# A routed expert layer: two gathers and two stores under way, a new order of issue on GpSimd, the router by token tiles, and the first expert loads in the norm before it

## The reference, cut to what matters

```python
p_group = softmax(h @ w_rg + b_rg)              # 4 groups, the best one is taken
p_top, g_idx = top_k(p_group, 1)
e_top, e_local = top_k(expert logits of that group, 2)   # 8 experts in a group
weights = p_top * softmax(e_top)
# each token's row goes to its two experts, in padded blocks of one expert
def expert_block(args):
    xb, e = args
    return (silu(xb @ w_gate[e]) * (xb @ w_up[e])) @ w_down[e]
out = sum over the two experts of weights * y
```

## Time and profile before

| what | us |
|---|---|
| median of 3 runs | 3223.88 (3222.1 to 3224.71) |
| the profiled execution, its time | 3233.42 |
| its span in the trace | 3231.7 |
| PE busy | 2530.7 (78%) |
| DVE, ACT, POOL busy | 1255.3, 944.7, 364.4 |
| mean granted PE clock | 0.879 of full |

### The profile page before, as it was taken

The page is one execution under the profiler, slowest core; times in us unless marked ns, Lnnn a source line. Parts: engine busy times, 40 slices in busy tenths (PEclk is TensorE's granted clock), DMA queues, the critical chain, the costliest instruction groups (busy, mean ns, idle before and its releaser), DMA issues. The chain is left out here.

```text
span 3231.7 us, 51558 instructions
## 1 busy us (share of the span) xinstructions
PE 2530.7 (78%) x17988; PEld 1959.7 (61%) x17989; DVE 1255.3 (39%) x2672; ACT 944.7 (29%) x1720; POOL 364.4 (11%) x706
## 2 busy tenths in 40 slices
PE   4974698589889859699898388894969998658883
PEld 4963688445445438476677266663847677636662
DVE  3447334311111145447443432235734753432224
ACT  2233323112112122236322133332234532213232
POOL 0000000012111110000000233231000000113233
PEclk9987899789999979799999598896979999768887
DMA  3201231489999942122121669944122121289972
GB/s 119 80 1 39 66 117 53 181 354 407 414 409 412 404 153 75 33 66 66 50 57 56 276 234 348 349 182 139 53 57 58 49 63 44 65 347 363 362 298 100
DMA packets 208903, 565.75 MB, mean 175 GB/s; under 512 B 26198, under 2 KB 170198, under 8 KB 184192
## 3 DMA queue, kind: packets, MB, share of 16 engines
q1 hardware_dynamic: 191056, 538.71, 45.1%
q0 software_dynamic: 17712, 25.23, 2.4%
HBM read 560.18 MB, written 35.92 MB: 184 GB/s over the span
## 5 line engine op out<-in xcount | busy, mean ns | idle before, releaser
L997 PE MATMUL ps<-e_wgu,e_xT 128*64 128x128 f32 (+1 forms) x2688 | 426.4, 321 | 41.2 <-issue 22.5
L997 PEld LDWEIGHTS ps<-e_wgu,e_xT 128*64 128x64 f32 x2688 | 344.4, 147 | 165.2 <-issue 116.7
L999 PE MATMUL ps<-e_wgu,e_xT 128*64 128x128 f32 (+1 forms) x2688 | 426.1, 321 | 0.0
L999 PEld LDWEIGHTS ps<-e_wgu,e_xT 128*64 128x64 f32 x2688 | 344.0, 147 | 0.0
L1020 PE MATMUL ps<-e_wd,e_hidT 128*64 128x512 f32 x1112 | 303.8, 682 | 5.4 <-ACT e_hidT L1051 4.0
L1903 PE MATMUL ps<-t_hT,t0a_t0g_w 128*128 128x512 f32 x768 | 199.2, 411 | 4.6 <-DVE t0a_t0g_w L1925 2.4
L1903 PE MATMUL ps<-t_hT,t1a_t1g_w 128*128 128x512 f32 x768 | 198.0, 409 | 4.6 <-DVE t1a_t1g_w L1925 2.4
L1162 DVE COPY e_y_out<-e_y 128x512 f32<-128x512 f32 x108 | 46.3, 429 | 372.9 <-DMA e_dram_y<-e_y_out,e_choicecur 267.4
L447 POOL TENSOR_TENSOR all_x<-all_x,ln_rows 128x1024 f32<-128x1024 f32 x16 | 48.2, 3040 | 1262.5 <-DVE all_x L440 1262.5
L1170 DVE TENSOR_TENSOR e_hid<-e_silu,ps 64x128 f32<-64x128 f32 (+1 forms) x210 | 67.1, 334 | 299.5 <-ACT e_silu L1048 293.0
L1048 ACT ACTIVATE e_silu<-ps 64x128 f32<-64x128 f32 (+1 forms) x210 | 63.9, 304 | 378.5 <-PE ps L999 377.5
(11 more groups left out here) (604 smaller groups left out, 4738.6 us busy)
## 6 DMA issues: line engine op xcount, KB each, us to landing
e_wgu<-in_w_exp_gate_up SPq DMA_DIRECT2D x54, 2048.0 KB, 9.2
e_wgu<-in_w_gate_up SPq DMA_DIRECT2D x22, 4096.0 KB
e_wd<-in_w_down SPq DMA_DIRECT2D x32, 2048.0 KB
e_wd<-in_w_exp_down SPq DMA_DIRECT2D x64, 1024.0 KB
m_both<-in_w_gate_up SPq DMA_DIRECT2D x10, 4096.0 KB, 37.8
r_hT<-in_w_exp_gate_up SPq DMA_DIRECT2D x10, 2048.0 KB
t0a_t0g_raw<-in_w_in SPq DMA_DIRECT2D x32, 512.0 KB
t1a_t1g_raw<-in_w_in SPq DMA_DIRECT2D x32, 512.0 KB
```

The source lines that it names most:

```text
L997: nc.tensor.matmul(ps_gu[q][0:SLOTS], xT[:, c, :], wgu[s][:, 0, c, span], start=c == 0, stop=c == DC - 1)
L999: last = nc.tensor.matmul(ps_gu[q][SLOTS:P], xT[:, c, :], wgu[s][:, 1, c, span], start=c == 0, stop=c == DC - 1)
```

## The change

- `ExpertRing` and `Router` are new: the ring of weights and the router's tiles belong to the stage around the norm and the expert layer. The norm's SP program loads the router and the first 2 (e0) or 5 (e1, e2) experts. In `moe` SP first stores the rows, and then, after the logits and the store, loads the last slot.
- The logits: 32 matmuls with a 128x128 tile of `hT` stationary and the router's 36 columns moving, no copy on ACT and no turning back.
- The counts have a semaphore of their own and are multiplied ahead of the ranks; the numbers of blocks come by rounding (3 instructions for 7). The tables that the loops read, the softmax weights and the scaling of x come later on DVE. `tokcol` comes ahead of `choicecol`, and POOL gathers as soon as `tokcol` is there; the small stores come behind two gathers, and are four.
- `landing` and `y` have two buffers each, `y_out` is gone; DVE copies the result from PSUM straight to `y`, ACT doesn't.
- DVE's order in block g: both `hid`, `xT`, the result's copy, `stage_rows`. PE turns the first half of the hidden rows ahead of the next block's rows.
- POOL goes by pairs of blocks, rounded up: store of block n, then gather of block n+3 into the buffer of block n+1. With an odd number of blocks one empty store and gather are added.
- The results come back tile by tile, both halves of a tile in turn.

```diff
@@ rms_rows / post_norm, SP @@
+                if ring is not None:
+                    ring.load_first(sp)
...
+                if router is not None:
+                    for dst, src in router.loads:
+                        sp.dma_start(dst, src).then_inc(router_landed, 16)
+                    ring.load_first(sp)
+                    sp.wait_ge(router_landed, 16 * len(router.loads))
@@ ExpertRing @@
+    def load_first(self, sp):
+        for s in range(self.n - 1):
+            for m in range(2):
+                self.load(sp, s, s, m)
@@ moe, SP @@
-                first = [(s, m) for s in range(RING) for m in range(2)]
-                for s, m in first[:EARLY]:
-                    load(s, s, m)
-
-                for n in range(EARLY, len(first)):
-                    if n == 2 * OWN:
-
-                        sp.wait_ge(logitsT_ready, 1)
-                        sp.wait_ge(rows_stored, 16)
-                    load(first[n][0], *first[n])
+                sp.wait_ge(logits_ready, 1)
+                sp.wait_ge(rows_stored, 16)
+                for m in range(2):
+                    ring.load(sp, RING - 1, RING - 1, m)
@@ moe, PE @@
-                pe.wait_ge(router_landed, 64)
-
-                for c in range(DC):
-                    last = nc.tensor.matmul(ps[0:NG + NE, 6, :], router[:, c, :], hT[:, c, :], start=c == 0, stop=c == DC - 1)
-                last.then_inc(logitsT_ready, 1)
-                pe.wait_ge(logitsT_copied, 1)
                 for t in range(TT):
-                    last = nc.tensor.transpose(ps[:, t, 0:NG + NE], logitsT[:, t * P:(t + 1) * P], ident[0:NG + NE, 0:NG + NE])
+                    for c in range(DC):
+                        last = nc.tensor.matmul(ps[:, t, 0:NG + NE], hT[:, c, t * P:(t + 1) * P], router.w[:, c, :],
+                                                start=c == 0, stop=c == DC - 1)
                 last.then_inc(logits_ready, 1)
...
+                        turn_hid(g, 0)
                         pe.wait_ge(rows_staged, g + 2)
                         turn()
...
+                        turn_hid(g, 1)
@@ moe, ACT @@
-                        act.wait_ge(y_ready, g + 1)
-                        act.wait_ge(y_moved, g + 1)
-                        nc.scalar.copy(y[:], ps_y).then_inc(y_copied, 1)
@@ moe, DVE @@
                         g = dve.snap(done)
-                        move_y(g)
                         for q in range(2):
                             dve.wait_ge(silu_ready, g * 2 + (q + 1))
                             vec.tensor_tensor(hid[SLOTS:P, q], silu[SLOTS:P, q], ps_gu[q][SLOTS:P], ALU.mult).then_inc(hid_ready, 1)
                         turn_copy(g + 2)
-                        stage_rows(g + 2)
+
+                        dve.wait_ge(y_stored[0], (g + 4) // 2 * 16)
+                        dve.wait_ge(y_stored[1], (g + 3) // 2 * 16)
+                        dve.wait_ge(y_ready, g + 1)
+                        vec.tensor_scalar(y[:, bass.ds(g % 2, 1)].rearrange("p one d -> p (one d)"), ps_y,
+                                          1.0, None, ALU.mult).then_inc(y_copied, 1)
+
+                        dve.wait_ge(rows_gathered[0], (g + 4) // 2 * 16)
+                        dve.wait_ge(rows_gathered[1], (g + 3) // 2 * 16)
+                        vec.tensor_scalar(gathered[:], landing[:, bass.ds(g % 2, 1)].rearrange("p one d -> p (one d)"),
+                                          1.0, None, ALU.mult).then_inc(rows_staged, 1)
@@ moe, POOL @@
-                        pool.wait_ge(rows_staged, g + 3)
-                        gather(g + 3)
-
-
-                        pool.wait_ge(y_moved, g + 2)
-                        nc.gpsimd.tensor_copy(choicecur[:], choicecol[:, bass.ds(g, 1)]).then_inc(choicecur_ready, 1)
+                with pool.Fori(0, n_pairs) as pair:
+                    for p in range(2):
+                        n = pair * 2 + p
+                        pool.wait_ge(y_copied, n + 2)
+                        store(n, p)
+                        pool.wait_ge(rows_staged, n + 2)
+                        gather(n + 3, 1 - p)
```

More of the change, by code:

```diff
@@ L318, in plain, with rms_rows @@
     return f
-def rms_rows(nc, name, parts, eps, loads=()):
+def rms_rows(nc, name, parts, eps, loads=(), ring=None):
     with Stage(nc, name) as st:
@@ L872, in moe @@
         y_copied = st.sem("y_copied")
-        y_moved = st.sem("y_moved")
-        y_stored = st.sem("y_stored")
+        y_stored = [st.sem(f"y_stored{n}") for n in range(2)]
         back_landed = [st.sem(f"back_landed{n}") for n in range(2 * TT)]
@@ L980, in turn, with turn_hid @@
                     last.then_inc(turned, 1)
+                def turn_hid(g, q):
+                    pe.wait_ge(hid_ready, g * 2 + (q + 1))
+                    for f in range(HF):
+                        last = nc.tensor.matmul(ps_hid[q][:, f * SLOTS:(f + 1) * SLOTS],
+                                                hid[SLOTS:P, q, f * P:(f + 1) * P], ident[SLOTS:P, SLOTS:P],
+                                                start=True, stop=True)
+                    last.then_inc(hid_turned, 1)
                 pe.wait_ge(rows_staged, 1)
@@ L1090, in _ @@
                 vec.tensor_copy(gpad[:, 0, 0:1], diff[:, 0:1]).then_inc(diff_ready, 1)
+                dve.wait_ge(counts_ready, 1)
+                blocks = rounded([nblk[:, n] for n in range(3)], ps[:, 5, 0:NE], 1.0 / SLOTS, 0.5 - 0.5 / SLOTS, 1.0)
+                link(vec.tensor_tensor_scan(ends[:, 0], blocks, blocks, 0.0, ALU.add, ALU.bypass))
+                link(vec.tensor_tensor(ends[:, 1], ends[:, 0], blocks, ALU.subtract))
+                link(vec.tensor_scalar(ends[:, 2], ends[:, 1], float(SLOTS), None, ALU.mult))
@@ new lines, in _ @@
+                dve.wait_ge(rank_ready, 1)
+                link(vec.tensor_tensor(slot[:], ps[:, 4, 0:TT * NE].rearrange("p (t e) -> p t e", e=NE),
+                                       ends[:, 2:3].to_broadcast([P, TT, NE]), ALU.add))
+                for j in range(2):
+                    link(vec.tensor_tensor(picked[:, j], slot[:], hot[:, j], ALU.mult))
+                link(vec.tensor_reduce(slotf[:], picked[:].rearrange("p j t e -> p (j t) e"), AX_X, ALU.add))
+                in_block = rounded([blk[:, n] for n in range(3)], slotf[:], 1.0 / SLOTS, 0.5 / SLOTS - 0.5)
@@ new lines, in _ @@
+                vec.tensor_tensor(flat, flat, k["choice"][:].rearrange("p j t -> p (j t)").unsqueeze(2).to_broadcast(
+                    [P, 2 * TT, TABLE]), ALU.mult).then_inc(hot_slots_ready, 1)
+                vec.tensor_copy(table[0:1, 0], blocks[0:1]).then_inc(table_ready, 1)
+                vec.tensor_copy(table[0:1, 1], ends[0:1, 0])
+                n_pairs = rounded([pairs[:, n] for n in range(3)], ends[0:1, 0, NE - 1:NE], 0.5, 0.25)
+                vec.tensor_copy(pair_table[:], n_pairs).then_inc(table_ready, 1)
@@ new lines, in _ @@
+                dve.wait_ge(tokT_ready, 1)
+                vec.tensor_scalar(part[:, 0], ps_tok, 1.0, float(4 * S + 2), ALU.is_lt, ALU.mult)
+                link(vec.tensor_scalar(part[:, 1], ps_tok, float(S), float(-S), ALU.is_gt, ALU.mult))
+                link(vec.scalar_tensor_tensor(part[:, 3], ps_tok, -1.0, part[:, 1], ALU.add, ALU.add))
+                vec.tensor_tensor(tokcol[:], part[0:SLOTS, 3], part[0:SLOTS, 0], ALU.add).then_inc(tokcol_ready, 1)
+                link(vec.tensor_scalar(part[:, 2], ps_tok, 2.0, k["second"][:], ALU.mult, ALU.add))
@@ L1134, in _ @@
-                vec.tensor_tensor(tokcol[:], part[0:SLOTS, 3], part[0:SLOTS, 0], ALU.add).then_inc(tokcol_ready, 1)
+                if alpha != 1.0:
+                    dve.wait_ge(rows_stored, 16)
+                    link(vec.tensor_scalar(x[:], x[:], alpha, None, ALU.mult))
                 def turn_copy(n):
@@ new lines, in _ @@
+                pool.wait_ge(rows_stored, 16)
+                pool.wait_ge(landing_cleared, 1)
+                pool.wait_ge(tokcol_ready, 1)
+                for n in range(2):
+                    gather(n, n)
+                for n in range(4):
+                    nc.gpsimd.dma_start(spare_dram[n:n + 1], ident[0:1, 0:SLOTS]).then_inc(y_stored[n % 2], 16)
+                pool.wait_ge(choicecol_ready, 1)
+                pool.wait_ge(rows_staged, 1)
+                gather(2, 0)
+                pool.wait_ge(table_ready, 2)
@@ L1229 @@
+                n_pairs = pairs_of_blocks(pool)
+                with pool.Fori(0, n_pairs) as pair:
[5 more added lines that the diff above has]
+                        gather(n + 3, 1 - p)
+                for n in range(2):
+                    pool.wait_ge(rows_gathered[n], n_pairs * 16 + 32 - 16 * n)
 class Columns:
```

317 lines of the change are left out of this document (136 added, 181 removed).

## The result

The changed kernel takes **3254.0 us** (median of 4 runs, 3248.5 to 3260.6) against 3223.0 before: ratio **1.0102**, interval 1.0075 to 1.0129. It is 31 us slower. The forecast was 3166, and the range ended at 3215. The profiled execution took 3260.6 us, span 3258.8, which is 27.1 us more span than before.

What follows compares the result with a forecast made beforehand. Weights bound e0's loop; in e1 and e2 PE waits for `hid`, with DVE late at a store. Prologues -43.5, loops -13 and -3, ends +1.7 sum to -58: median 3166 us, range 3105 to 3215.

Steps and rivals of the forecast that it cites:

- the term L: Expert loops: a gather's landing time behind a store, taken as 7.2 us, the mean of 6.2, 8.0 and 7.5.
- The sum for a pair: Loops of e1 and e2: two blocks take L + 8.5 us plus 2 x 1.33 for the clock, 18.4 in all.
- a gain of 13 us: Loops of e1 and e2: 9.2 us a block against 9.47, over some 48 blocks, -13 us.
- Rival B: Loops: the gather lands late behind its store, beside loads that never pause; L = 11, 3256 us; chance 0.09.
- the prologues at -43.5: Serial part ahead of each expert loop: e0 -14.4, e1 -14.8, e2 -14.3 us, sum -43.5.
- Rival C: Prologues: router matmuls stay at the lower clock, first gather still meets loads; -16 instead of -43.5, 3193 us; chance 0.17.
- Rival A: Loops: shorter stalls leave the clock up, loads then bound a block at 8.3 us; 56 us gained, 3123; chance 0.27.
- The logits: Router in the prologue: 22 records at the lower clock, 42 at the higher, 10.3 us; change 0, bounds -3.6 and +3.9 a layer.
- The early loads: Prologue: weights loaded from the norm on shorten the first gather's landing by 5.0, 4.5, 4.0 us; rows stored behind them cost nothing.
- e0's counts in full: e0's prologue gain of 14.4 us counts whole, since 430 us of saturated loading follow.
- The end: End of each layer: -0.7 us each without ACT, up to +3.8 for e2's empty store and gather; sum +1.7.

Runs made afterwards that it cites:

- Experiment 10: Changed kernel, but in e1 and e2 the next expert's gate-and-up load is issued at an expert's last block's end, with the down load: 3221.5 us, ratio 0.9976.
- experiment 3: Light loads: ring refills bring only 1/16 of gate and up and 1/16 of down (1/32 in e0), store still ahead of gather: 2953.3 us, one run.
- experiment 2: Changed kernel with the gather issued ahead of the store, but both waits kept ahead of both issues: 3154.0 us, ratio 0.9791.
- experiment 9: Changed kernel with e2's stores issued but all half rows except one out of bounds, results read back from the stored rows: 3257.0 us, one run.
- experiment 8: On top of experiment 1, the first experts' loads moved back into the expert layer, behind the rows' store: 3127.5 us, ratio 0.9702.
- Experiment 4: The changed kernel's new prologue with the loop of before (one landing buffer, result copied by ScalarE, gather ahead of store): 3187.6 us, ratio 0.9903.
- experiment 1: Changed kernel with gather n+3 issued ahead of the store of block n, without waiting for that block's end: 3110.8 us, ratio 0.9656.

## Why the prediction was wrong

**The loop's structure was right, the term L was mis-sized.** The sum for a pair was L + 8.5 + 2.65. With the measured L it gives 9.07 + 11.15 = 20.2 us in e1 and 9.67 + 11.15 = 20.8 in e2. Measured: 20.1 in the pair above, where what is not L took 11.4, and as the median of all pairs with a stall over 3 us 19.9 in e1 and 21.0 in e2. The stall in every second block, the waits for `landing` and the end of the wait for the store all came as written. What failed is "I take their mean, 7.2". The value came from gathers of before, issued at any distance from a load; the new order fixes that distance within 1 us of a load, where L was longest in before too (8.9 us). Experiment 10 shows this for 1.4 and 1.6 us, and experiment 3 that nothing of it is left with light loads. The 0.7 to 0.9 us of experiment 2 don't add to this: there the gather moved past the store and away from the load at once, and experiment 9 leaves 0.3 us for the store. Of the remaining 0.5 and 0.9 us over 7.2, 0.5 and 0.3 are an error of the choice itself: three rows gave a mean of 7.2 where all of before's waited gathers give 7.75 and 7.5. That accounts for e1; about 0.6 us of e2's L stays open.

**The point of indifference was nearer than it looked.** At 9.47 us a block before, the pair breaks even at L = 7.8. I gave this loop a gain of 13 us with L only 0.6 below that, and a rival at L = 11 with a chance of 0.09, deciding at 9.6. The measured 9.1 lies between 7.8 and 9.6, and 9.7 above both: 10.0 and 10.5 us a block, half of the median pairs. Also, 9.47 is the rate of one stretch of e2. From the third to the 33rd interval between copies to `xT`, a block took 8.97 us before in e1 and in e2, and 9.82 and 9.92 after, so I had compared with too slow a value. With the measured L the prediction's 48 blocks give +38 instead of -13; the two loops were 46.7 us longer.

**Rival B** named the right mechanism (the gather lands late, in loads that never pause) and came out at 3256, close to the 3254 measured. That closeness is luck: it had L at 11 and the prologues at -43.5, and both were off, in opposite directions. **Rival C** was right in both its parts: the logits ran nearly all at the lower clock (+9.1 us over three layers, 64 records at 0.20 us each, where it had 14.4) and the first gather still met loads (8.2 us less gained than forecast, where it had 13). B's and C's mechanisms happened together, which I had treated as alternatives. **Rival A**'s mechanism showed only where the stall was made shorter (experiment 2).

**The logits.** I had put 42 of the 64 records at the higher clock. In e1 all 64 ran at a granted 0.50, 1.2 GHz, as the window above shows. In e0 the clock was still up from the turning of the rows when they began (0.90 from 605 to 608 us, then 0.85, the first 11 records in 1.34 us), and it fell to 0.50 while PE was busy with them without a pause, and stayed there; PE took 13.04 us. So it did not rise on this work, and it did not hold on it either; why is not known. I had argued from e0's turning, 32 other matmuls; no row of before showed the clock over so many matmuls like these, and the upper bound, +3.9 us a layer, was the one to lean to.

**The early loads.** "Whether they wait for them or not, they land by 628 in e0, ahead of POOL's need at 638, so this costs nothing": SP went on behind them at 631.98, still ahead of the gather. But I had not asked who else waits for them. SP does, with the last slot behind it, so that slot was loaded from 1824.0 to about 1835 in e1, just beside the first gather at 1830.4. The late store had been judged harmless by POOL's need alone; the queue that waited was SP's own. Against before the landing gained 5.3 us instead of 13.5. Against a kernel without early loads, which was not the comparison that I made, they give 12 us (experiment 8).

**"e0's counts in full"** did not come true in the changed kernel: the prologue gave 8.9 us and the loop took 6.2 back. In before the DMA engines were busy up to the first block; window of before:

```profile
652.00:662.00 10.00, 1.26 (x9) 1.24 (x9) 0.69 (x1) 0.00 (x0) 0.74 (x3) 0.50 0.99 372
```

In the changed kernel the same window is at 0.04, as shown above: the ring was full and the loads stood until block 0 freed a slot. The first refill still came 10.2 us sooner (662.6 instead of 672.8). Experiment 4 has the same prologue and the same pause, with the old loop; its windows:

```profile
652.00:662.00 10.00, 8.73 (x57) 5.69 (x59) 2.56 (x5) 0.38 (x1) 2.77 (x6) 0.64 0.08 23
690.00:1120.00 430.00, 372.87 (x2758) 215.38 (x2756) 73.91 (x142) 90.22 (x171) 79.24 (x174) 0.94 1.01 409
```

There e0's prologue took 61.9 us and its loop 495.6, 10.5 us less together than before: the early start counted in full. So the 6.2 us lie in the new loop, as far as one profile of each kernel can say: in the nine kernels with it and full loads e0's loop took 497.2 to 504.6 us, 501.6 on average. In the changed kernel its loads ran at 405 GB/s instead of 410 over 430 us (1.2%, 5 us). Why the rate was lower was not tried.

**The end** came as forecast: +2.4 us in e2, with its odd 33 blocks, and -0.5 in e1.

## What to carry to other kernels

A second buffer gives a transfer its lead only if the queue that issues it doesn't stand ahead of it for something later: put the issue whose buffer comes free first in front, and count in which block each wait ends (store first +31 us, gather first -113 us, with the same buffers). When a rearrangement ties a small transfer to an event, look at what else that event issues; a latency measured at mixed phases is no value for a fixed one. And before a gain is written down, work out the value of the doubtful term at which it vanishes, and give the side beyond it a chance that fits the spread of the rows.

The best version is experiment 1 with the logits transposed, 3104.4 us, 0.9623 of before (0.9602 to 0.9645); against experiment 1 alone (0.9656, 0.9622 to 0.9690) the difference is not settled.

## What the hardware showed that I had not expected

- A 2.1 MB store behind 15.7 MB of loads landed after 26.6 us, and on another engine's queue after 23.4, against 8.3 when issued ahead of them.
- A gather of 64 rows lands in 3.7 us with light loads beside it, in 7.4 beside full loads that are issued over 1 us away from it, and in 9.3 when issued within 1 us of a 2 MB load; the bytes of a store ahead of it are worth 0.3 us.
- The 64 matmuls of e1's logits, 13.8 us of busy PE in 18, ran at a granted clock of 0.50 from first to last. In e0, where the clock was up when they began, it fell from 0.85 to 0.50 under them, with PE busy throughout.
